# Expert matrices loaded with four neighbouring rows to a partition, and one-hot rows made a step sooner

## The chip, the cores and the metric

The kernel runs on one core of one Trainium2 chip. The time is that of the device in microseconds (us), the median of several runs; before the change it is 1736.42 us, the median of three (1735.65 to 1737.06).

## What is computed

Two blocks in a row on 256 tokens of 1024 features, in float32. The first (two layers of retention, dilated attention, gated mixing and a gated feed-forward) and most of the second (a state-space branch and a pooling branch with modulation by a condition vector) are touched by the change only through small loads. The change acts on the end of the second block, a mixture of experts:

```python
xl = post_norm(xl, mod_l[2] * out_l, ln1_g, ln1_b)          # layer_norm(alpha * x + y)
hl = modulate(xl, mod_l[3], mod_l[4])                        # x * (1 + scale) + shift
lg = hf @ w_rg + b_rg;  grp = argmax(lg)                     # one of 4 groups of 8 experts
le = (hf @ w_re[grp] + b_re[grp]);  top_v, top_i = top_k(le, 2)
w = softmax(lg)[grp] * softmax(top_v)
# each token goes to its 2 experts of 32:
def swiglu(xb, wg, wu, wd):                                  # wg, wu: 1024 x 512, wd: 512 x 1024
    return (silu(xb @ wg) * (xb @ wu)) @ wd
y = segment_sum(swiglu(...)[dest] * w, token)
xl = post_norm(xl, mod_l[5] * y, ln2_g, ln2_b)
```

## The kernel before

Everything is one program in which each of the five engines has its own function (`tensor`, `scalar`, `vector`, `gpsimd`, `sync`) with the order of its work written out by hand. Work is ordered across engines by named marks on semaphores: `then(..., key)` or `sig(...)` sets a mark when an instruction is done, `wait_ge(*at(key))` waits for it. Almost all instructions are recorded in small helpers, so a line in the profile says which kind of operation it is: L143 is a matmul, L145 a transpose on TensorE, L147 an activation, L149 tensor_tensor, L151 tensor_scalar, L153 scalar_tensor_tensor, L159 a copy, L169 a DMA issue.

**The expert stage.** The 32 experts are taken in 16 pairs. At most 64 tokens of each expert are handled in a round (`CAP`), and the tokens of the two experts of a pair stand side by side as 128 columns. For pair p:
- VectorE's `gather` makes one-hot rows `ONE` (which token stands at which place; four tensor_scalar of 128x64) and `PW`, the same with the token's weight (four more).
- TensorE's `gather` multiplies the normed tokens `X` with `ONE`: eight blocks of 128 features, in two banks (q = 0 and 1), each block as four instructions, and transposes `PW`. VectorE (q = 0, two operations) and ScalarE (q = 1, four) apply the modulation and leave the features on the partitions in `HG`.
- TensorE's `gate_up` multiplies `HG` with the gate matrices of both experts (part 0), then with the up matrices (part 1). Between the two it does `combine(p - 1)`, which adds the previous pair's result, spread over the tokens by `PWT`, and VectorE's `combined` accumulates it in `YA`.
- VectorE multiplies silu(gate) with up into `AV`; TensorE transposes `AV` in four blocks; VectorE copies them into `AT`; TensorE's `down` multiplies with the down matrices; VectorE scales the result into `OE`.

The order on TensorE is gate(p), combine(p-1), up(p), gather(p+1), transposes of the products of p, down(p). The order on VectorE is combined(p-1), `AV`, then all of `gather(p+1)` with its one-hot rows first, then the copy into `AT`, then `OE`.

**The matrices.** Each expert has three matrices of 2 MB: pair p needs loads k = 6p to 6p+5 (gate, gate, up, up, down, down). They go in turn into nine slots of 16 KB a partition (`expert_slots`). Loads 0 to 7 are issued by ScalarE during the stages before, load 8 and on by SP (`expert_loads`), each as soon as the matmuls that read the slot before are done: two loads when gate(p) is done, two when up(p) is done, two when down(p) is done. The source is read as `(k p) n -> p k n`: partition p holds rows p, 128+p, 256+p, and so on, so a gate or up matrix arrives as 1024 rows of 512 floats and a down matrix as 512 rows of 1024 floats.

**Before the experts.** `layer_norm` (VectorE: subtract and scale, times gain, plus bias on the second half of the features; GpSimd: plus bias on the first half) works in place on `X`. `routing` transposes `X` and multiplies with the router's weights `WR`, which GpSimd's `small_loads` loaded early in the first layer. The modulation vectors `modc` come from a product with `w_ada_2` and a bias that stands in `colT`.

Of the kernel before, what the change touches and what calls it, by code (L numbers as in the profile page):

```python
# [287 lines left out]
def program(nc, A, out):  # L288
    st = ExitStack()
    with st:  # L290
# [71 lines left out]
        s_col = [sem("col0_in"), sem("col1_in"), sem("col0b_in")]  # L362
# [107 lines left out]
        GSA, GSB = view(0, 8, 256), fold(ring[:, SLOT:SLOT + 2048], 8)  # L470
        dcol, ghalf, bhalf = stat[:, 128:144], stat[:, 144:160], stat[:, 240:256]
# [21 lines left out]
        PT1 = view(8192, 2, 512)  # L493
        BN = stat[:, 160:184].rearrange("p (t a b) -> p t a b", t=2, a=2)
# [63 lines left out]
        def expert_load(e, r, k):  # L558

            p, j = divmod(k, 6)  # L560
            name = ("w_expert_gate_2", "w_expert_up_2", "w_expert_down_2")[j // 2]
            src = A[name][0, 2 * p + j % 2].rearrange("(k p) n -> p k n", p=P)
            e.dma_start(fold(slot_for(r, k), 8 if j < 4 else 4), src).then_inc(*landed(s_w[r][k % len(s_w[r])], ("ew", r, k)))
# [3 lines left out]
        def tensor(t):  # L567
# [45 lines left out]
            def layer(l):  # L613
# [205 lines left out]
                def ada_sums(u):  # L819
                    bk = take(("ada", u), ("modc", u))  # L820
                    t.wait_ge(*at("am", u, "kept"))
                    if u // 2 in (2, 5):
                        t.matmul(bk, C("selbc"), AD[u % 2], True, True).then_inc(*sig(s_mm, ("ada", u)))
                        return
                    for c in range(4):
                        made = t.matmul(bk[:, 2 * c:2 * c + 2], AD[u % 2][:, tok(c)], C("selc"), True, True)
                    made.then_inc(*sig(s_mm, ("ada", u)))
# [332 lines left out]
            def routing():  # L1160
                bkl = take(("lg",), ("lg", "kept"), hold=True)
                for i in range(2):
                    for q in range(2):
                        bk = take(("hm", i, q), ("hm", i, q, "kept"))
                        for h in range(2):
                            t.wait_ge(*at("ln", 1, i, h))
                        for k in range(4):
                            made = t.transpose(bk[:, tok(k)], X[:, i, tok(4 * q + k)], ident)
                        made.then_inc(*sig(s_turn, ("hm", i, q)))
                    t.wait_ge(*at("wrg_in"))  # L1170
                    t.wait_ge(s_small[6], 64)
# [12 lines left out]
            def experts(r, s_done):  # L1184

                def gather(p):
                    i = p % 2
                    for q in range(2):
                        bk = take(("hg", r, p, q), ("hg", r, p, q, "kept"))
                        t.wait_ge(*at("one", r, p))  # L1190
                        for k in range(4):
                            c = tok(4 * q + k)
                            made = summed(bk[:, tok(k)], [(X[:, x, c], ONE[:, i, x, :]) for x in range(2)])
                        made.then_inc(*sig(s_done, ("hg", r, p, q)))
                    bk = take(("pw", r, p), ("pw", r, p, "kept"))
                    t.wait_ge(*at("pwd", r, p))
                    for x in range(2):
                        made = t.transpose(bk[:, tok(x)], PW[:, i, x, :], ident)
                    made.then_inc(*sig(s_done, ("pw", r, p)))

                def gate_up(p):
                    i = p % 2
                    for part in range(2):
# [5 lines left out]
                        t.wait_ge(*at("hg", r, p, 0, "kept"))  # L1209
                        t.wait_ge(*at("hg", r, p, 1, "kept"))  # L1210
                        for k in range(8):
                            t.matmul(bk[0:64, :], HG[:, i, k, 0:64], wa[:, k, :], k == 0, k == 7)
                            made = t.matmul(bk[64:128, :], HG[:, i, k, 64:128], wb[:, k, :], k == 0, k == 7)
# [4 lines left out]
                def down(p):  # L1218
                    i = p % 2
# [4 lines left out]
                    made.then_inc(*sig(s_done, ("av", r, p)))  # L1224
                    k0 = 6 * p + 4
# [519 lines left out]
        def vector(v):  # L1745
# [118 lines left out]
            def modulated_by(u):  # L1864
# [9 lines left out]
                then(v.tensor_tensor(o, fold(bk[:, 0:8], 4), bc(colT[:, 2, 4 * u:4 * u + 4], 2), ALU.add), *([] if plus else [("modc", u)]))  # L1874
# [451 lines left out]
            def layer_norm(name, tiles, x):  # L2326
# [7 lines left out]
                for i in tiles:  # L2334
# [3 lines left out]
                    for h in range(2):  # L2338
                        then(v.tensor_tensor(x[:, i, half(h)], x[:, i, half(h)], GB[:, 0, half(h)], ALU.mult), ("lng", name, i, h))
                    v.wait_ge(*at("ln_row", name, 1))  # L2340
                    v.wait_ge(*v.latest)
                    then(v.tensor_tensor(x[:, i, half(1)], x[:, i, half(1)], GB[:, 1, half(1)], ALU.add), ("ln", name, i, 1))
# [104 lines left out]
            def experts(r, s_done):  # L2447
# [9 lines left out]
                def gather(p):  # L2457
# [14 lines left out]
                    then(made, ("pwd", r, p))  # L2472
                    o = HG[:, i, 0:4, :]
# [7 lines left out]
                def combined(p):  # L2481
                    for x in range(2):
                        for h in range(2):
                            y, bk = YA[:, x, half(h)], B("ya", r, p, h, x)
                            v.wait_ge(*at("ya", r, p, h, x))
                            if r == 0 and p == 0:
                                then(v.stt(y, X[:, x, half(h)], ALPHA, bk, ALU.mult, ALU.add), ("ya", r, p, h, x, "kept"))
# [7 lines left out]

                gather(0)
                for p in range(16):
                    i = p % 2
                    if p:
                        combined(p - 1)  # L2500
# [4 lines left out]
                    then(v.tensor_tensor(AV, SIL, B("gu", r, p, 1), ALU.mult), ("gu", r, p, 1, "kept"), ("av_made", r, p))  # L2505
# [46 lines left out]
        def gpsimd(g):  # L2552
# [34 lines left out]
            def small_loads():  # L2587
# [7 lines left out]
                g.dma_start(WR[:, :, 0:4], A["w_router_group_2"][0].rearrange("(k p) n -> p k n", p=P)).then_inc(*landed(s_small[5], ("wrg_in",)))  # L2595
                for k in range(4):
                    g.dma_start(WR[:, :, 4 + 8 * k:12 + 8 * k], A["w_router_expert_2"][0, k].rearrange("(k p) n -> p k n", p=P)).then_inc(*landed(s_small[6]))
# [83 lines left out]
            def layer_norm(name, tiles, x):  # L2681
                i0, i1 = tiles[0], tiles[-1] + 1
                power(RV[:, i0:i1], i1 - i0, ("var", name, i0), ("rstd", name, i0))
                for i in tiles:
                    g.wait_ge(*at("ln_row", name, 1))
                    g.wait_ge(*at("lng", name, i, 0))
                    then(g.tensor_tensor(x[:, i, half(0)], x[:, i, half(0)], GB[:, 1, half(0)], ALU.add), ("ln", name, i, 0))
# [14 lines left out]
            g.dma_start(colrow[0:48, 2, :], fl(A["b_ada_2"][0])).then_inc(*landed(s_col[1]))  # L2702
            layer(0)
# [200 lines left out]
```

## Time and profile before

| | |
|---|---|
| Median of 3 runs | 1736.42 us |
| The profiled execution | 1734.91 us, span 1733.0 us |
| TensorE busy | 1623.3 us, 94% |
| VectorE, ScalarE, GpSimd busy | 45%, 34%, 27% |
| Read from HBM | 395.15 MB, 229 GB/s over the span |
| Expert stage | from about 1222 us to the end |

Times inside the profile are microseconds from the span's start. PE is TensorE's matmuls, PEld its weight loads, DVE is VectorE, ACT ScalarE, POOL GpSimd, SP the engine that issues most DMAs; SPq, ACTq are their queues. `ps<-arena` names what is written and read: `ps` is PSUM, `arena`, `ring` and `rows` are the large tensors in SBUF in which the named views lie (`ring` and parts of `arena` and `rows` hold the nine slots). A float32 matmul shows as two instructions.

### The profile page before, as it was taken

The page shows a single profiled execution, that of the slowest core. Times are in us where ns is not written, and L with a number is a line of the kernel's source. Part 1 is how long each engine was busy: PE and PEld are TensorE (multiplying, and loading weights), DVE is VectorE, ACT ScalarE, POOL GpSimd, SP SyncE. Part 2 cuts the span into 40 slices and gives each one's busy share as a digit, 9 for nine tenths or more (in the row PEclk, how much of TensorE's full clock was granted, in tenths as well). Part 3 has the DMA queues.
Part 4 walks back from the last instruction along what each step waited for, and adds up shares of the span by engine and source line. Part 5 has one row for each costly group of instructions (what it writes and reads, how often), then busy time and mean ns, then how long its engine had stood idle before and what let it go on. Part 6 is the DMA issues. An engine that isn't in the chain of part 4 may idle for free.

```text
span 1733.0 us, 23951 instructions
## 1 busy us (share of the span) xinstructions
PE 1623.3 (94%) x9717; PEld 1212.2 (70%) x9717; DVE 773.7 (45%) x1320; ACT 584.6 (34%) x1046; POOL 463.0 (27%) x291
## 2 busy tenths in 40 slices
PE   7999999989999999989999999996899999989996
PEld 5888998869889888878768888985434343343342
DVE  4644433266443332697756564466222222222323
ACT  3543444335434444555445564331100000000000
POOL 3532554433325444100245563432000000000000
PEclk9999999999999999999999999997999999999998
DMA  7644996545449874333223437569699999999992
GB/s 256 213 136 132 265 245 219 174 166 162 137 137 292 248 267 170 107 85 95 68 74 98 107 114 241 166 201 339 232 391 397 392 393 396 392 394 395 392 395 101
DMA packets 305444, 397.83 MB, mean 230 GB/s; under 512 B 6565, under 2 KB 195265, under 8 KB 304944
## 3 DMA queue, kind: packets, MB, share of 16 engines
q1 hardware_dynamic: 293424, 365.45, 63.3%
q10 hardware_dynamic: 9136, 20.85, 3.3%
q0 software_dynamic: 2768, 9.93, 1.7%
q8 instruction: 80, 1.31, 0.3%
q14 instruction: 36, 0.29, 0.1%
HBM read 395.15 MB, written 1.05 MB: 229 GB/s over the span
## 4 chain that ended last, share of the span: by engine, by line
PE 83%; DVE 10%; DMA 3%; issue 2%; ACT 1%; POOL 1%; SPq 0%; DVEq 0%; ACTq 0%; POOLq 0%
PE ps L143 81%; DVE arena L153 2%; DVE arena L149 2%; PE ps L145 2%; DVE split_r L149 2%; DMA ring<-in_w_branch_b 1%; DVE arena L159 1%; ACT split_r L147 1%; DVE arena L151 1%; DMA ring<-in_w_in 1%; DMA X<-in_x 0%; ACT arena L147 0%; DVE X L153 0%; POOL split_r L149 0%; POOL stat L149 0%
## 5 line engine op out<-in xcount | busy, mean ns | idle before, releaser
L143 PE MATMUL ps<-arena_r,split_r 128*128 128x256 f32 (+1 forms) x2984 | 462.0, 289 | 5.8 <-ACT split_r L147 3.3
L149 POOL TENSOR_TENSOR split_r<-ring,split_r 128x1024 fp32r<-128x1024 f32 (+1 forms) x142 | 334.3, 2356 | 336.9 <-ACT split_r L147 327.8
L143 PEld LDWEIGHTS ps<-arena_r,split_r 128*128 128x128 f32 x2984 | 395.5, 189 | 23.1 <-issue 14.4
L147 ACT ACTIVATE split_r<-ring 128x1024 fp32r<-128x1024 f32 (+1 forms) x293 | 296.0, 1019 | 300.5 <-PE ps L143 213.2
L143 PE MATMUL ps<-arena 128*64 128x512 f32 (+7 forms) x1472 | 359.6, 491 | 10.1 <-DVE arena L159 5.0
L149 DVE TENSOR_TENSOR split_r<-ring,split_r 128x1024 fp32r<-128x1024 f32 (+1 forms) x151 | 214.1, 1420 | 312.6 <-ACT split_r L147 304.8
L143 PE MATMUL ps<-split_r,arena_r 128*128 128x512 f32 (+1 forms) x1520 | 342.5, 378 | 2.9 <-issue 1.7
L143 PEld LDWEIGHTS ps<-split_r,arena_r 128*128 128x128 f32 x1520 | 274.7, 188 | 51.5 <-issue 8.2
L143 PEld LDWEIGHTS ps<-arena 128*64 128x64 f32 (+2 forms) x1472 | 154.5, 156 | 169.8 <-issue 147.0
L143 PE MATMUL ps<-ring,arena 128*64 128x512 f32 (+2 forms) x768 | 211.2, 576 | 12.2 <-DVE arena L159 8.6
L143 PE MATMUL ps<-hhh_r,split_r 128*128 128x256 f32 (+1 forms) x976 | 222.7, 317 | 0.0
L147 ACT ACTIVATE arena<-ps 128x256 f32<-128x256 f32 (+4 forms) x182 | 76.6, 435 | 357.2 <-PE ps L143 352.0
L149 DVE TENSOR_TENSOR arena<-arena,ps 128x512 f32<-128x512 f32 (+1 forms) x124 | 73.4, 592 | 259.4 <-PE ps L143 224.2
L143 PEld LDWEIGHTS ps<-hhh_r,split_r 128*128 128x128 f32 x976 | 162.9, 190 | 12.2 <-issue 0.6
L143 PEld LDWEIGHTS ps<-ring,arena 128*64 128x64 f32 (+1 forms) x768 | 75.2, 143 | 114.3 <-issue 92.0
L169 POOL DMA_DIRECT2D rows<-in_ln_g x2 | 1.2, 608 | 490.7 <-PE ps L143 490.7
L147 ACT ACTIVATE arena<-ps,modc 128x128 f32<-128x128 f32 x92 | 34.5, 457 | 258.2 <-PE ps L143 235.9
L143 PE MATMUL ps<-arena,X 128*128 128x128 f32 x640 | 81.2, 286 | 35.9 <-DVE arena L151 35.9
L143 PEld LDWEIGHTS ps<-arena,X 128*128 128x128 f32 x640 | 77.2, 200 | 50.8 <-DVE arena L151 39.1
L149 DVE TENSOR_TENSOR arena<-ps,rows 128x512 f32<-128x512 f32 x60 | 40.7, 690 | 132.4 <-PE ps L143 131.9
L153 DVE SCALAR_TENSOR_TENSOR arena<-ps,rows,arena 128x508 f32<-128x508 f32 (+4 forms) x104 | 69.7, 675 | 26.8 <-ACT arena L147 20.3
L149 POOL TENSOR_TENSOR arena_r<-arena,arena_r 128x256 fp32r<-128x256 f32 (+1 forms) x46 | 38.2, 832 | 159.6 <-ACT arena_r L147 151.2
(144 smaller groups left out, 1144.7 us busy)
## 6 DMA issues: line engine op xcount, KB each, us to landing
ring<-in_w_gate_up SPq DMA_DIRECT2D x88, 512.0 KB, 7.3
arena<-in_w_expert_up SPq DMA_DIRECT2D x15, 2048.0 KB, 19.2
arena<-in_w_expert_gate SPq DMA_DIRECT2D x15, 2048.0 KB, 20.1
ring<-in_w_expert_down SPq DMA_DIRECT2D x15, 2048.0 KB, 19.7
ring<-in_w_in SPq DMA_DIRECT2D x57, 512.0 KB, 5.3
ring<-in_w_expert_gate SPq DMA_DIRECT2D x13, 2048.0 KB, 16.6
arena<-in_w_ada SPq DMA_DIRECT2D x24, 1024.0 KB, 7.1
ring<-in_w_down SPq DMA_DIRECT2D x22, 1024.0 KB, 4.9
```

The source lines that it names most:

```text
L143: made = e.matmul(*a, **k)
L145: made = e.transpose(*a, **k)
L147: made = e.activation(*a, **k)
L149: made = e.tensor_tensor(*a, **k)
L151: made = e.tensor_scalar(*a, **k)
L153: made = e.scalar_tensor_tensor(**k)
L159: made = e.tensor_copy(*a, **k)
L169: made = e.dma_start(*a, **k)
```

## The change

Three things are changed. Expert matrices are read as `(q p k) n -> p q (k n)` with k = 4 (gate, up) and `(p k) n -> p (k n)` (down): four neighbouring rows to a partition, 8 KB or 16 KB in one piece. For this the features of the tokens are stored reordered: the norm before the experts writes `X` so that block k of a half holds features 4p+k, and the router's weights, the modulation bias and the product `AV` are reordered alike; the accumulation of pair 0 puts the order back. The one-hot rows of pair p+1 are made at the beginning of step p. And TensorE turns the products of p between the two halves of gather(p+1).

```diff
         def expert_load(e, r, k):
-            src = A[name][0, 2 * p + j % 2].rearrange("(k p) n -> p k n", p=P)
-            e.dma_start(fold(slot_for(r, k), 8 if j < 4 else 4), src).then_inc(...)
+            w = A[name][0, 2 * p + j % 2]
+            if j < 4:
+                o, src = fold(slot_for(r, k), 2), w.rearrange("(q p k) n -> p q (k n)", q=2, k=4)
+            else:
+                o, src = slot_for(r, k), w.rearrange("(p k) n -> p (k n)", k=4)
+            e.dma_start(o, src).then_inc(...)
...
+        in_fours = lambda x: x.rearrange("t (k p) -> t p k", k=4)
+        by_four = lambda x: x.rearrange("t (p k) -> t p k", k=4)
...
 # tensor: experts
-                gather(0)
+                for q in range(2):
+                    gather(0, q)
                 for p in range(16):
                     gate_up(p)
                     if p < 15:
-                        gather(p + 1)
+                        gather(p + 1, 0)
+                    turn_products(p)
+                    if p < 15:
+                        gather(p + 1, 1)
                     down(p)
...
 # vector: layer_norm (gain goes to LT, the add writes X reordered; gpsimd the same for half 0)
-                        then(v.tensor_tensor(x[:, i, half(h)], x[:, i, half(h)], GB[:, 0, half(h)], ALU.mult), ...)
+                        then(v.tensor_tensor(LT[i][:, half(h)], x[:, i, half(h)], GB[:, 0, half(h)], ALU.mult), ...)
-                    then(v.tensor_tensor(x[:, i, half(1)], x[:, i, half(1)], GB[:, 1, half(1)], ALU.add), ...)
+                    then(v.tensor_tensor(in_fours(x[:, i, half(1)]), by_four(LT[i][:, half(1)]), by_four(GB[:, 1, half(1)]), ALU.add), ...)
...
 # vector: experts (ones_of is the one-hot part of the former gather)
+                ones_of(0)
                 gather(0)
                 for p in range(16):
                     i = p % 2
+                    if p < 15:
+                        ones_of(p + 1)
                     if p:
                         combined(p - 1)
...
-                    then(v.tensor_tensor(AV, SIL, B("gu", r, p, 1), ALU.mult), ...)
+                    then(v.tensor_tensor(in_fours(AV), by_four(SIL), by_four(B("gu", r, p, 1)), ALU.mult), ...)
...
 # gpsimd: small_loads (five loads of the router's weights become ten)
-                g.dma_start(WR[:, :, 0:4], A["w_router_group_2"][0].rearrange("(k p) n -> p k n", p=P))...
-                for k in range(4):
-                    g.dma_start(WR[:, :, 4 + 8 * k:12 + 8 * k], A["w_router_expert_2"][0, k].rearrange("(k p) n -> p k n", p=P))...
+                for q in range(2):
+                    rows_of = lambda x: x[512 * q:512 * q + 512].rearrange("(p k) n -> p k n", k=4)
+                    g.dma_start(WR[:, 4 * q:4 * q + 4, 0:4], rows_of(A["w_router_group_2"][0]))...
+                    for k in range(4):
+                        g.dma_start(WR[:, 4 * q:4 * q + 4, 4 + 8 * k:12 + 8 * k], rows_of(A["w_router_expert_2"][0, k]))...
...
+            g.dma_start(fold(BP, 4), A["b_ada_2"][0][3 * D:5 * D].rearrange("(u p k) -> p u k", u=4, k=4))...
```

Left out above: the first accumulation reads `X` and the product with the same two reorderings; `ada_sums` and `modulated_by` take reordered weights and the bias `BP` for the eight modulation blocks that the experts use; TensorE waits for the two halves of `HG` separately.

## Rows read from the trace of the kernel before

**Rows 1.** The page: busy time by engine, and GB/s in 40 slices

```profile
PE 1623.3 (94%) x9717; PEld 1212.2 (70%) x9717; DVE 773.7 (45%) x1320; ACT 584.6 (34%) x1046; POOL 463.0 (27%) x291
...
GB/s 256 213 136 132 265 245 219 174 166 162 137 137 292 248 267 170 107 85 95 68 74 98 107 114 241 166 201 339 232 391 397 392 393 396 392 394 395 392 395 101
```

**Rows 2.** Chain that ended last, expert stage: start us, us, what

```profile
1424.19 0.69 DVE arena L149
1425.59 3.84 PE ps L143 x32
...
1430.86 24.63 PE ps L143 x104
1455.58 0.69 DVE arena L149
...
1708.90 8.16 PE ps L143 x34
```

**Rows 3.** Waits, 1230 to 1733: us in total, times, longest us

```profile
PE ps L143 <- DVE arena L151: 22.7, 15, 1.5
...
PE ps L143 <- DVE arena L159: 12.5, 16, 0.8
```

**Rows 4.** Timeline of one step: start us, us, engine, line, operation, out<-in

```profile
1424.79 1.62 DVE L151 TENSOR_SCALAR arena<-cst_sb,arena 128x64 f32<-128x64 f32 x8
...
1425.59 3.84 PE L143 MATMUL ps<-arena,X 128*128 128x128 f32 x32 [1.51 <-DVE arena L151]
1427.67 0.69 DVE L149 TENSOR_TENSOR arena<-ps,modc 128x512 f32<-128x512 f32 x1 [1.25 <-PE ps L143]
1428.40 0.69 DVE L149 TENSOR_TENSOR arena<-arena,modc 128x512 f32<-128x512 f32 x1
...
1429.26 0.82 PE L145 MATMUL ps<-cst_sb,arena 128*128 128x128 f32 x6
...
1430.12 0.69 DVE L159 COPY arena<-ps 128x512 f32<-128x512 f32 x1 [1.02 <-PE ps L145]
```

**Rows 5.** Windows of 3 us: busy by engine, PEclk, DMA share, GB/s

```profile
1418.00:1421.00 3.00, 3.00 (x18) 1.00 (x16) 0.00 (x0) 0.00 (x0) 0.00 (x0) 1.00 1.05 386
...
1466.00:1469.00 3.00, 3.00 (x16) 1.01 (x14) 0.65 (x1) 0.00 (x0) 0.00 (x0) 1.00 1.02 408
```

**Rows 6.** Timeline of SP's DMA issues in the expert stage

```profile
1228.90 0.37 SPq L169 DMA_DIRECT2D arena<-in_w_expert_up  x1
...
1298.95 13.84 SPq L169 DMA_DIRECT2D ring<-in_w_expert_gate  x2
...
1585.18 12.51 SPq L169 DMA_DIRECT2D ring<-in_w_expert_gate  x2
```

**Rows 7.** DMA packets between 1200 and 1733

```profile
DMA packets 78114, 189.19 MB, mean 355 GB/s; under 512 B 1529, under 2 KB 1529, under 8 KB 78084
```

**Rows 8.** Window of 1 us in which constants (1344 KB, 10.5 KB a partition) land

```profile
18.00:19.00 1.00, 1.00 (x5) 0.60 (x4) 0.86 (x6) 0.98 (x2) 0.00 (x0) 1.00 1.02 430
```

**Rows 9.** Timeline of VectorE before the experts: slowest 128x512, a norm's end

```profile
1165.52 2.48 DVE L149 TENSOR_TENSOR arena_r<-arena,arena_r 128x512 fp32r<-128x512 f32 x1 [0.71 <-ACT arena_r L147]
...
1196.23 2.96 DVE L149 TENSOR_TENSOR X<-X,rows 128x512 f32<-128x512 f32 x3
```

**Rows 10.** Timeline of GpSimd in the first layer

```profile
55.34 3.49 POOL L169 DMA_DIRECT2D small<-in_w_router_expert  x4
58.85 3.64 POOL L149 TENSOR_TENSOR split_r<-ring,split_r 128x768 fp32r<-128x768 f32 x2
66.53 2.59 POOL L149 TENSOR_TENSOR split_r<-ring,split_r 128x768 fp32r<-128x768 f32 x1 [4.04 <-ACT split_r L147]
```

**Rows 11.** Chain that ended last, stage before the experts

```profile
1128.13 5.49 DMA ring<-in_w_branch_b
...
1138.75 12.76 DMA ring<-in_w_branch_b
```

More of the change, by code:

```diff
@@ L1169, in routing @@
                         made.then_inc(*sig(s_turn, ("hm", i, q)))
[L1170 to L1171 removed]
+                    t.wait_ge(s_small[5], 32)
+                    t.wait_ge(s_small[6], 128)
                     for k in range(8):
@@ L1184, in experts, with gather @@
             def experts(r, s_done):
-                def gather(p):
+                def gather(p, q):
                     i = p % 2
-                    for q in range(2):
-                        bk = take(("hg", r, p, q), ("hg", r, p, q, "kept"))
-                        t.wait_ge(*at("one", r, p))
-                        for k in range(4):
-                            c = tok(4 * q + k)
-                            made = summed(bk[:, tok(k)], [(X[:, x, c], ONE[:, i, x, :]) for x in range(2)])
-                        made.then_inc(*sig(s_done, ("hg", r, p, q)))
+                    bk = take(("hg", r, p, q), ("hg", r, p, q, "kept"))
+                    t.wait_ge(*at("one", r, p))
+                    for k in range(4):
+                        c = tok(4 * q + k)
+                        made = summed(bk[:, tok(k)], [(X[:, x, c], ONE[:, i, x, :]) for x in range(2)])
+                    made.then_inc(*sig(s_done, ("hg", r, p, q)))
+                    if q == 0:
+                        return
                     bk = take(("pw", r, p), ("pw", r, p, "kept"))
@@ L1216, in gate_up, with turn_products @@
                             combine(p - 1)
-                def down(p):
-                    i = p % 2
+                def turn_products(p):
                     bk = take(("av", r, p), ("av", r, p, "kept"))
@@ L1224, in down @@
                     made.then_inc(*sig(s_done, ("av", r, p)))
+                def down(p):
                     k0 = 6 * p + 4
@@ L1873, in modulated_by @@
                 plus = u // 2 in (1, 4)
-                then(v.tensor_tensor(o, fold(bk[:, 0:8], 4), bc(colT[:, 2, 4 * u:4 * u + 4], 2), ALU.add), *([] if plus else [("modc", u)]))
+                added_to = colT[:, 2, 4 * u:4 * u + 4]
+                if u // 2 in (3, 4):
+                    v.wait_ge(*at("bp_in"))
+                    added_to = BP[:, 4 * u - 24:4 * u - 20]
+                then(v.tensor_tensor(o, fold(bk[:, 0:8], 4), bc(added_to, 2), ALU.add), *([] if plus else [("modc", u)]))
                 if plus:
@@ L2338, in layer_norm @@
                     for h in range(2):
-                        then(v.tensor_tensor(x[:, i, half(h)], x[:, i, half(h)], GB[:, 0, half(h)], ALU.mult), ("lng", name, i, h))
+                        then(v.tensor_tensor(LT[i][:, half(h)], x[:, i, half(h)], GB[:, 0, half(h)], ALU.mult), ("lng", name, i, h))
                     v.wait_ge(*at("ln_row", name, 1))
                     v.wait_ge(*v.latest)
-                    then(v.tensor_tensor(x[:, i, half(1)], x[:, i, half(1)], GB[:, 1, half(1)], ALU.add), ("ln", name, i, 1))
+                    then(v.tensor_tensor(in_fours(x[:, i, half(1)]), by_four(LT[i][:, half(1)]), by_four(GB[:, 1, half(1)]), ALU.add), ("ln", name, i, 1))
             def first_norm(i):
@@ L2455, in experts, with ones_of @@
                 v.wait_ge(*v.latest)
-                def gather(p):
+                def ones_of(p):
                     i = p % 2
@@ L2472, in gather @@
                     then(made, ("pwd", r, p))
+                def gather(p):
+                    i = p % 2
                     o = HG[:, i, 0:4, :]
@@ L2486, in combined @@
                             if r == 0 and p == 0:
-                                then(v.stt(y, X[:, x, half(h)], ALPHA, bk, ALU.mult, ALU.add), ("ya", r, p, h, x, "kept"))
+                                then(v.stt(by_four(y), in_fours(X[:, x, half(h)]), ALPHA, by_four(bk), ALU.mult, ALU.add), ("ya", r, p, h, x, "kept"))
                             else:
@@ L2686, in layer_norm @@
                     g.wait_ge(*at("lng", name, i, 0))
-                    then(g.tensor_tensor(x[:, i, half(0)], x[:, i, half(0)], GB[:, 1, half(0)], ALU.add), ("ln", name, i, 0))
+                    then(g.tensor_tensor(in_fours(x[:, i, half(0)]), by_four(LT[i][:, half(0)]), by_four(GB[:, 1, half(0)]), ALU.add), ("ln", name, i, 0))
             def norm_rows(name, a, b):
@@ L2702, in gpsimd @@
             g.dma_start(colrow[0:48, 2, :], fl(A["b_ada_2"][0])).then_inc(*landed(s_col[1]))
+            g.dma_start(fold(BP, 4), A["b_ada_2"][0][3 * D:5 * D].rearrange("(u p k) -> p u k", u=4, k=4)).then_inc(*landed(s_col[3], ("bp_in",)))
             layer(0)
```

21 lines of the change are left out of this document (12 added, 9 removed).

## The prediction

> **What bounds the kernel now.** I began with the page. TensorE is busy in 94% of the span, but over the last eleven of the 40 slices, where the experts run, the DMA engines move 391 to 398 GB/s, far above the 230 GB/s mean [rows 1]. So there are two candidates for the bound in that stage, and the stage is where the change acts. The chain of waits of the expert stage settles who sets the end: it repeats one pattern per pair of experts, from 1424.19 to 1455.58, a step of 31.39 us, and in it there is no transfer at all: 24.63 us of down, gate, combine and up matmuls, then VectorE, then the gather, then VectorE again [rows 2]. The totals of waits say the same: TensorE waits 22.7 us in 15 waits for the one-hot rows (L151) and 12.5 us in 16 waits for the copy of the turned products (L159) [rows 3]; no wait for a transfer is in that answer. A reader should see one step in the timeline [rows 4]: the eight one-hot operations start at 1424.79, behind the product of gate and up, and the gather starts at 1425.59 when the first four are done, 1.5 us after the up matmuls ended; the transposes start at 1429.26 and take 0.82, and the copy at 1430.12 holds TensorE for another 0.78.
>
> But the transfers are close behind. In stretches in which only gate and up matrices land (rows of 512 floats, 2 KB) the rate is 386 GB/s; where only down matrices land (4 KB rows) it is 408 [rows 5]. A pair is six matrices of 2.097 MB, 12.58 MB: 4 x 5.43 + 2 x 5.14 = 32.0 us, against a step of 31.39. The transfers are therefore already 2% too slow, and the kernel lives on its lead of nine slots. The issues on SP show it: the same two gate issues come at 1298.95 and, nine steps later, at 1585.18, which is 286.2 us where nine steps are 282.5; SP has slipped 3.7 us because the queue is full [rows 6]. So neither half of this change is enough alone, and this is the point of the prediction: with a shorter step on TensorE the old transfers would become the bound, and with faster transfers alone nothing would happen.
>
> **The change part by part.**
> *One-hot rows a step sooner, gather in two halves around the turning of the products.* The one-hots of the next pair now run before the combine, during the down matmuls, so the 15 waits of 1.51 go: 22.7 us. In the new order TensorE goes from up directly to half of the gather, 16 instructions, half of 3.84 = 1.92 us. The product of gate and up (0.69) ends by then, with 1.1 us to spare. Then come the four turns, the other half, and the two turns of the weights: all of it 3.84 + 0.82 = 4.66 us from the end of up. VectorE's work meanwhile: its two operations on the first gathered half start 2.08 after the gather's start (1427.67 against 1425.59) and end 1.42 later [rows 4], at 3.5, and the copy (0.69) ends at 4.2, before 4.66. So the second wait is covered too, with 0.4 us to spare: 15 x 0.78 = 11.7 us. (The 16th, in the last pair, stays: no gather is left there.) Together 34.4 us. Back-to-back groups of matmuls still have about 0.1 us between them where the wait was, 15 x 0.1 = 1.5. This leaves 32.9 us. The new step is 31.39 - 2.2 = 29.2 us.
> *The transfers.* 29.2 us for 12.58 MB asks for 431 GB/s. What do rows of 8 KB (gate, up) and 16 KB (down) give? All packets of the stage are of 2 or 4 KB [rows 7], so I draw a line through the two rates. Per engine, 2048 bytes take 16 x 2048 / 386 = 84.9 ns and 4096 take 16 x 4096 / 408 = 160.6; a fixed part of 9.2 ns and 75.7 per 2 KB. Then 8 KB take 312 ns (420 GB/s) and 16 KB take 615 (426): an estimate, 422 GB/s over a pair, 29.8 us. The nearest row to it is the microsecond in which rows of 10.5 KB (constants) land, 430 [rows 8]; the bound below is the present mix, 393 (12.58 MB in 32.0 us). With 422 the transfers are slower than TensorE by 0.6 us a step, 9 us in 15 steps, and the nine slots hold that: the first load behind the preloaded ones is issued at 1228.90 [rows 6], 87 loads or 182.5 MB are left, and the last must be there when the last down matmuls start, at 1708.90 [rows 2] less 31.9, 1677. That needs 182.5 / (1677 - 1231) = 409 GB/s. At 422 the last lands at about 1664. So at 409 or more TensorE alone sets the end.
>
> *The reordering of features.* The second half of a norm's add (VectorE), the first half (GpSimd), the product (16 times) and the first accumulation now write with 512 bytes between neighbours. No row shows such a write. Below, they cost nothing more than now; above, I take the slowest VectorE operation on 128x512 in the trace, 2.48 us, for 0.69 [rows 9]. At 2.48 the product would end 0.6 us after the half gather, 15 x 0.6 + 1.8 in the last pair = 11 us, and two norm adds in the chain would add 2 x 1.8 = 3.6. The three VectorE operations behind a norm take 2.96 together now [rows 9]. I take 0.5 us for the norm and nothing for the product, as 1.1 us of cover absorbs a 2.5-fold duration.
>
> The rule that speaks against the change is in the Trainium skill, Advanced Engine Details and Errata, section Memory Cachelines: an access that leaves its 16-byte line each time pays a penalty, with no size given. No row of this trace shows such a write. By the rule the time would be nearer to the second rival's 1718 than to 1704.5.
>
> *Small loads.* Five more issues on GpSimd: four such take 3.49 us now, two operands' low parts (3.64) stand behind them [rows 10]. The halves are smaller, so 5 x 0.5 to 5 x 0.87: 2.5 to 4.4 us of delay, once, on an engine that idles 4.04 us soon after [rows 10]; 0 to 2 us, I take 0.5. The bias load is one issue of 0.5 us, far from its use.
> *The preloaded matrices.* Eight of them share the engines with the last weights before the experts. One such load lies in the chain beside an expert's matrix: 12.76 us, where its like took 5.49 alone [rows 11]. It waits for the whole matrix already (5.4 us), so longer packets can't make it much worse: -7.3 to +2, I take 0.
>
> Sum: 34.4 - 1.5 - 0.5 - 0.5 = 31.9 us. Of the profiled execution (1734.91, span 1733.0) this leaves 1703.0, span 1701.1. The median of the runs is 1.5 above it: 1736.42 - 31.9 = 1704.5.
>
> **The rivals.**
> *Rows are cut or are no faster (12 in 100).* The descriptors stay at today's rates, the one-hots' gain is real. TensorE's 29.2 outruns 393 GB/s, the lead is used up at about the tenth pair, and then each pair waits some 2.8 us for its gate matrices. The last load lands at 1231 + 182.5 / 0.393 = 1695, and the last down starts there, 13 to 16 us before 1708.90: 1720 to 1723. For it: only two lengths were seen in this stage. Against: [rows 8].
> *Strided writes are dear (11 in 100).* As worked out, 31.9 - 14 = 18 gained: 1718.
> *Slower: long rows hurt the memory side (6 in 100).* Sixteen engines read neighbouring 8 KB pieces of one matrix at once, instead of 2 KB pieces, and meet in the same banks. Below 182.5 / (1708.90 - 1231) = 382 GB/s the time is above today's, and at 360 the last load lands at 1738, 29 us late: 1765. Against: [rows 8], and that 4 KB beat 2 KB.
> *More than forecast (6 in 100).* The preloaded matrices let the weights through sooner, up to 7 us: 1697.
>
> **How the numbers follow.** Forecast 65 in 100, 1704.5, itself 1700 to 1710. The range of 1697 to 1722 takes in the strided writes and most of the first rival and leaves out about 12 in 100. A measurement of this kernel can tell 0.2%, 3.5 us. Faster 0.92: all but the slower case and 2 in 100 for the first two rivals at once, which together take back nearly all; same 0.02, for these; slower 0.06.
>
> **What would show it.** The chain of the expert stage has steps of 29.2 us, with neither L151 nor L159 among its waits but for the first and the last pair; packets of the stage of 8 KB and over, rates of 418 to 428 GB/s; no wait of TensorE for a matrix; SP no longer held for 6.9 us by an issue (13.84 for two now, [rows 6]). A wait for an expert's matrix from the middle pairs on would say that the first rival holds; L149 before the turns, that the writes are dear.

## The result, and the profile after

The changed kernel takes 1708.16 us (median of 4 runs, 1706.24 to 1713.51), the kernel before beside it 1736.74 (4 runs, 1735.65 to 1738.08): ratio 0.984, 95% interval 0.9817 to 0.9863. Forecast were 1704.5 in a range of 1697 to 1722. The gain is 28.6 us instead of 31.9. The profiled execution took 1707.69 us, span 1705.8, against a span of 1733.0 before.

The page of the changed kernel, for [rows 1]: busy time, and GB/s in 40 slices.

```profile
PE 1627.1 (95%) x9717; PEld 1214.9 (71%) x9717; DVE 779.8 (46%) x1320; ACT 584.7 (34%) x1046; POOL 468.0 (27%) x297
...
GB/s 259 206 135 133 253 266 213 184 119 200 141 91 300 249 250 228 127 77 99 75 50 100 101 108 135 297 170 260 166 415 421 424 421 421 424 422 425 421 424 119
```

Ten slices that stood at 391 to 397 now stand at 415 to 425. In the expert stage the chain, for [rows 2], holds nothing but TensorE from the second pair to the last:

```profile
1418.60 0.44 PE ps L145 x4
1419.04 1.79 PE ps L143 x16
...
1421.04 26.51 PE ps L143 x120
1447.56 0.44 PE ps L145 x4
```

A step is 28.96 us (31.39 before). The waits of TensorE from 1230 on, for [rows 3]; the two that are left are those of the last pair:

```profile
PE ps L145 <- DVE arena L149: 1.2, 1, 1.2
PE ps L143 <- DVE arena L159: 0.8, 1, 0.8
```

The timeline of one step, for [rows 4]:

```profile
1445.51 2.05 PE L143 MATMUL ps<-arena,X 128*128 128x128 f32 x16
...
1445.69 1.05 DVE L149 TENSOR_TENSOR arena<-arena,ps 128x512 f32<-128x512 f32 x1 [6.41 <-PE ps L143]
...
1447.39 0.60 PE L145 MATMUL ps<-cst_sb,arena 128*128 128x128 f32 x4
1447.59 0.69 DVE L149 TENSOR_TENSOR arena<-ps,modc 128x512 f32<-128x512 f32 x1 [0.85 <-PE ps L143]
1447.83 1.95 PE L143 MATMUL ps<-arena,X 128*128 128x128 f32 x16
...
1448.93 0.68 DVE L159 COPY arena<-ps 128x512 f32<-128x512 f32 x1
```

The strided product takes 1.05 us where it took 0.69, and ends at 1446.74, before the transposes at 1447.39. The copy ends at 1449.61; the down matmuls that read it start at 1449.93. Both waits are covered, as forecast.

But the chain has a new piece ahead of the experts, in the norm:

```profile
1180.29 17.11 DMA rows<-in_ln_b
...
1197.42 1.04 DVE X L149
```

The timeline of VectorE says the same, for [rows 9]; the norm stands still for its gain (2.07 us) and then for its bias (4.98 us):

```profile
1191.14 1.29 DVE L149 TENSOR_TENSOR arena<-X,rows 128x512 f32<-128x512 f32 x2 [2.07 <-DMA rows<-in_ln_g]
1197.42 1.04 DVE L149 TENSOR_TENSOR X<-arena,rows 128x512 f32<-128x512 f32 x1 [4.98 <-DMA rows<-in_ln_b]
```

The span divides at two marks: the start of the last norm's first operation, and the gather of pair 0. All columns are worked out from the traces' times. The first column moves by itself: in the 14 profiles an operation of GpSimd near 500 us, with the same code ahead of it but for the small loads, starts between 498.5 and 504.8.

| kernel | start to norm | norm and routing | experts | span |
|---|---|---|---|---|
| before | 1180.96 | 33.77 | 518.27 | 1733.0 |
| after | 1182.95 | 40.64 | 482.21 | 1705.8 |
| difference | +1.99 | +6.87 | -36.06 | -27.2 |

So the experts gave 36.1 us, more than forecast, and 8.9 were lost ahead of them, where I had put 1.0. The experiments take these three columns in turn.

### The profile page after: what moved, and what is told of

Same layout as the page of the kernel before. It is cut to its first block, busy times and chain, and to the rows that moved or that the text cites. A ratio compares the mean times of both kernels' runs of the same rounds, so it can differ in the third digit from the quotient of the medians.

```text
span 1705.8 us, 23942 instructions
## 1 busy us (share of the span) xinstructions
PE 1627.1 (95%) x9717; PEld 1214.9 (71%) x9717; DVE 779.8 (46%) x1320; ACT 584.7 (34%) x1046; POOL 468.0 (27%) x297
## 3 DMA queue, kind: packets, MB, share of 16 engines
HBM read 395.16 MB, written 1.05 MB: 232 GB/s over the span
## 4 chain that ended last, share of the span: by engine, by line
PE 86%; DVE 7%; issue 3%; DMA 2%; POOL 2%; ACT 1%; ACTq 0%; DVEq 0%; POOLq 0%
PE ps L143 84%; DVE arena L153 2%; PE ps L145 2%; DVE arena L149 1%; DVE split_r L149 1%; DMA rows<-in_ln_b 1%; POOL split_r L149 1%; POOL small L169 1%; DMA ring<-in_w_in 1%; DMA X<-in_x 0%; ACT split_r L147 0%; ACT arena L147 0%; DVE X L153 0%; DVE arena L159 0%; POOL arena_r L149 0%
## 5 line engine op out<-in xcount | busy, mean ns | idle before, releaser
L143 PE MATMUL ps<-ring,arena 128*64 128x512 f32 (+2 forms) x768 | 214.7, 584 | 4.4 <-DVE arena L149 2.4
L149 DVE TENSOR_TENSOR arena<-arena,ps 128x512 f32<-128x512 f32 (+1 forms) x124 | 79.4, 640 | 235.3 <-PE ps L143 200.4
L143 PEld LDWEIGHTS ps<-arena,X 128*128 128x128 f32 x640 | 77.3, 198 | 27.3 <-issue 23.8
```

The source lines that it names most:

```text
L143: made = e.matmul(*a, **k)
L149: made = e.tensor_tensor(*a, **k)
```

## The experiments

Theory: TensorE's two waits are gone because of the order, long rows are what lets the transfers keep up, and the loss ahead of the experts has two causes of its own. In the table, each kernel's median against the kernel before in the same study, and the stretches of its profiled execution.

| kernel | median us | ratio, 95% interval | norm | experts |
|---|---|---|---|---|
| order_only | 1728.9 | 0.9955 (0.9942 to 0.9969) | 33.71 | 510.51 |
| old_order | 1751.1 | 1.008 (1.0056 to 1.0104) | 40.78 | 520.90 |
| late_ones | 1737.4 | 1.001 (0.9996 to 1.0025) | 40.69 | 510.05 |
| whole_gather | 1723.4 | 0.9912 (0.9884 to 0.994) | 40.78 | 494.50 |
| short_all | 1734.2 | 0.9991 (0.9977 to 1.0004) | 37.82 | 510.79 |
| rows_late | 1737.4 | 1.0007 (0.9995 to 1.0019) | 40.78 | 509.90 |
| rows_4_4 | 1723.4 | 0.9935 (0.9918 to 0.9952) | 39.77 | 492.53 |
| rows_4_16 | 1715.4 | 0.9891 (0.9873 to 0.9908) | 40.38 | 487.30 |
| rows_first8 | 1706.1 | 0.982 (0.9796 to 0.9844) | 34.35 | 482.47 |
| early_rows | 1704.0 | 0.9811 (0.9788 to 0.9833) | 34.35 | 482.54 |
| ada_copy | 1705.0 | 0.982 (0.9793 to 0.9847) | 40.07 | 482.08 |
| best | 1699.3 | 0.9783 (0.9757 to 0.9808) | 34.35 | 481.75 |

### The two halves of the change, each alone

**Order alone.** The kernel before with only its order changed (`ones_of(p + 1)` ahead of `combined(p - 1)`, `turn_products(p)` between the two halves of the gather), rows of 2 and 4 KB and features in the old order.

> The kernel before with the change of order alone: one-hot rows a step sooner, the products turned between the two halves of the gather; matrices still in rows of 2 and 4 KB, features not reordered. Theory (both halves are needed): TensorE's step could be 28.96 us, but the transfers give 393 GB/s, so after some ten pairs TensorE waits for gate matrices, 2 to 3 us a pair; gain 13 to 17 us, about 1721. Rival (the transfers had room, the long rows bring nothing): the whole gain of the expert stage, 36 us, about 1701.

Measured 1728.86 (1726.28 to 1730.47), a gain of 7. Its chain, where it goes over from TensorE to the transfers:

```profile
1411.71 12.36 PE ps L143 x57
1424.07 26.02 DMA ring<-in_w_expert_gate
```

The waits of TensorE in its expert stage:

```profile
PE ps L143 <- DMA ring<-in_w_expert_gate: 9.9, 5, 2.6
PE ps L143 <- DMA arena<-in_w_expert_gate: 8.9, 3, 3.7
```

Steps are 28.96 us until 1411, the seventh pair; then come waits for gate matrices, as the prediction's first rival describes, but three pairs sooner than it puts them. The mechanism is right; the gain is only half of what I expected (below).

**Long rows alone.** The changed kernel in the old order, on both engines:

```diff
                     if p < 15:
                         gather(p + 1, 0)
+                        gather(p + 1, 1)
                     turn_products(p)
-                    if p < 15:
-                        gather(p + 1, 1)
```

and `ones_of(p + 1)` back behind the product.

> The changed kernel with the old order: one-hot rows behind the product, both halves of the gather before the products are turned; long rows and reordered features stay. Theory (TensorE sets the step, transfers alone bring nothing): steps of 31.4 us and the losses before the experts stay, so 1708.2 + 36.4 = about 1744, slower than the kernel before. Rival (the transfers held the old kernel): little lost against the changed kernel, 1708 to 1715.

Measured 1751.07 (1748.78 to 1752.91): 15 us slower than before the change. Its chain around the product:

```profile
1439.44 1.03 DVE arena L149
1440.47 0.58 DVE arena L151 x4
...
1446.37 24.63 PE ps L143 x104
...
1471.09 1.03 DVE arena L149
```

The step is 31.65 where the old one was 31.39: the strided product takes 0.35 more, which nothing covers in this order, and the four one-hot operations in the chain 0.09 less (0.58 for 0.67). The experts lose 2.6 us by this against the kernel before. The rest of the loss stands ahead of them: 7.0 us in the norm, 3.9 in the modulation (both below), and some 4.5 us that this profile lost elsewhere ahead of the norm. Expected were 1744; the kernel is 7 us above that, 2.3 of them in the experts. So neither half is worth much alone (-7 and +15 us), and together they bring 28.6.

### Which of the two waits brings how much

**One-hot rows late, gather halved**: only `ones_of(p + 1)` moved back behind the product.

> The changed kernel (long rows, gather in two halves around the turns) with the one-hot rows of the next pair made behind the product of gate and up again, where they were before the change. This prices the first wait alone. Theory: TensorE waits for the first one-hots in each of 15 steps, 1.51 us as before the change and 0.35 more because the product in front of them writes strided and takes 1.04 instead of 0.69: 15 x 1.86 = 27.9, 1736 us and steps of 30.8; the second wait stays covered (the copy is ready 0.4 us before the second half of the gather ends). Rival: the two waits are one, what is not waited for at the first is waited for at the second, and taking the one-hots early alone brings less than 1.51 a step: 1725 or below.

Measured 1737.37 (1735.66 to 1741.19). The chain:

```profile
1402.70 0.58 DVE arena L151 x4
...
1403.32 2.05 PE ps L143 x16
...
1434.11 2.05 PE ps L143 x16
```

Steps of 30.79, 1.83 more than in the changed kernel, which is 27.5 us in 15 steps; the stage is 27.84 us longer, against 27.9 worked out.

**One-hot rows early, gather whole**: only `gather(p + 1, 1)` moved ahead of `turn_products(p)`.

> The changed kernel (long rows, one-hot rows early) with the whole gather in front of the turns of the products again. This prices the second wait alone. Theory: TensorE waits for the copy of the turned products in each step, 0.78 us, nothing else changes since the strided product has 3.8 us of cover: 15 x 0.78 = 11.7, 1720 us and steps of 29.75. Rival: the two halves bring no more than they cost (an extra switch between gather and turns, 0.1 us twice a step): 1708 to 1711.

Measured 1723.36 (1719.4 to 1726.58). The chain:

```profile
1403.48 0.67 PE ps L145 x6
...
1404.18 0.70 DVE arena L159
...
1404.92 28.37 PE ps L143 x136
1433.29 0.67 PE ps L145 x6
```

Steps of 29.81, 0.85 more, which is 12.8 us in 15 steps; the stage is 12.3 us longer, against 11.7. The two waits are separate and their prices add up: 1.83 + 0.85 = 2.68 a step, and old_order, which has both waits, is 2.69 a step above the changed kernel.

### The transfers

**Short rows again, as four transfers for each matrix.** The changed kernel with every matrix in four `dma_start` of one row to a partition and block.

> The changed kernel, but every matrix is loaded in four transfers that take one row of each partition, so the packets are 2 and 4 KB again while features and order stay as changed. Theory: the expert stage is bound by 393 GB/s or a little less, 20 us longer than in the changed kernel; the waits for the norm's rows before the experts (2.1 and 5.0 us) go, since nothing long stands in their way; about 1722 to 1727. Rival (packet length has no part): 1708 or, if the norm's rows come sooner, 1701.

Measured 1734.22 (1729.18 to 1740.54), more than expected. The edit has a side effect that I had missed: the two last matrices loaded beforehand are now eight issues on ScalarE, in front of the activations that the routing waits for. From its timeline:

```profile
1195.61 11.71 ACTq L169 DMA_DIRECT2D ring<-in_w_expert_gate  x8
1207.36 2.90 ACT L147 ACTIVATE arena<-ps,modc 128x128 f32<-128x128 f32 x8 [21.93 <-issue]
```

So the run can't price the rows alone, and three others replace it, with one transfer for each matrix, whose source is read in shorter rows (`(q p k) n -> p q (k n)` with k = 1 or 2). Their matrices don't stand in the order of the features, so their results aren't those of the computation; bytes, matmuls and order of work are the same.

**Rows of 2 and 4 KB from k = 8 on.**

```diff
+            if k >= 8:
+                if j < 4:
+                    o, src = fold(slot_for(r, k), 8), w.rearrange("(q p k) n -> p q (k n)", q=8, k=1)
+                else:
+                    o, src = fold(slot_for(r, k), 4), w.rearrange("(q p) n -> p q n", p=P)
```

> The changed kernel, but all loads from k = 8 on are read in rows of 2 and 4 KB as before the change (so wrong features, same work). It is the run with four times as many transfers without their side effect on ScalarE. Theory: transfers bind at 393 GB/s; 182.5 MB take 464 us where the stage leaves 444 between the first of these issues and the last down matmuls: 20 us late, and some 7 more as in the kernel with the new order alone: 1728 to 1735. Rival: the long rows are not what lets the stage run at 28.96 a step, the landing time of a single transfer or the lead does: 1708 to 1715.

Measured 1737.43 (1736.81 to 1739.4), 2.4 us above the range that the theory gave. The stage takes 509.90, nearly that of order_only (510.51).

**Rows of 4 KB for gate and up, 16 KB for down.**

> The changed kernel, but gate and up matrices from k = 8 on are read in rows of 4 KB (wrong features, same work), down matrices in 16 KB as now. Theory, from the line through the rates of packets (408 GB/s at 4 KB, 426 at 16 KB): 4 x 5.14 + 2 x 4.92 = 30.4 us a pair, 414 GB/s, and 182.5 MB take 441 us of the 444 there are: no loss, 1708 to 1710. Rival: the slots are too few for transfers that are 1.4 us a pair slower than TensorE, and waits come up from the middle pairs on: 1715 to 1722.

Measured 1715.39 (1713.73 to 1718.16), the rival's number but not its waits from the middle pairs on. The timeline of TensorE has one wait for a gate and one for an up matrix, both in the last pair:

```profile
1663.70 10.72 PE L143 MATMUL ps<-arena 128*64 128x512 f32 x40 [1.69 <-DMA arena<-in_w_expert_gate]
1676.48 8.79 PE L143 MATMUL ps<-arena 128*64 128x512 f32 x32 [2.07 <-DMA arena<-in_w_expert_up]
```

**Rows of 4 KB for all.**

> The changed kernel, but all matrices from k = 8 on are read in rows of 4 KB (gate and up with wrong features, same work). Theory: 408 GB/s, 182.5 MB take 447 us of the 444 there are: 3 us late and a little of the landing time, 1711 to 1716, so that two neighbouring rows to a partition would have been nearly enough. Rival: as soon as TensorE waits for transfers it loses more than the deficit, since the time in which a full ring stands still is not made up: 1718 or more.

Measured 1723.38 (1719.18 to 1725.15), again the rival's number. The rates of the four kernels, from the counts of packets between 1245 and 1640, in the order rows_late, rows_4_4, rows_4_16, after, a fence each:

```profile
DMA packets 63912, 155.67 MB, mean 394 GB/s; under 512 B 1188, under 2 KB 1188, under 8 KB 63894
```

```profile
DMA packets 40634, 161.57 MB, mean 409 GB/s; under 512 B 1238, under 2 KB 1238, under 8 KB 40615
```

```profile
DMA packets 31196, 163.95 MB, mean 415 GB/s; under 512 B 1255, under 2 KB 1255, under 8 KB 27832
```

```profile
DMA packets 18139, 167.02 MB, mean 423 GB/s; under 512 B 1271, under 2 KB 1271, under 8 KB 1271
```

The line through two rates gave 408, 414 and 422 for the last three. The rates are right within 1 GB/s; what was wrong is the rate that is needed. The stage takes 509.9, 492.5, 487.3 and 482.2 us; 182.5 MB at the first three rates are 463.2, 446.2 and 439.8 us, and what remains is 46.7, 46.3 and 47.5, nearly a constant: the stage lasts as long as the transfers and 47 us. TensorE's own 482.2 then ask for 182.5 / 435 = 419 GB/s, not 409. Changed kernel 423: 1% to spare.

### The loss ahead of the experts

**Gain and bias rows issued earlier.** GpSimd's waits and `norm_rows(1, ...)` moved ahead, in front of two of its tensor operations and of the operand splits behind them. The issue of the gain stands at 1109.79 where it was at 1179.67, 70 us sooner.

> The changed kernel with the two transfers of the first norm's gain and bias issued some 60 us sooner, in the gap after the branch_a weights, so that they don't share the engines with experts' matrices. Theory (the bias row's transfer, 10.0 us before and 17.1 after, was held up by the long packets of the preloaded matrices, and this cost 6.9 us): the waits of 2.1 and 5.0 us go, 1701 to 1702. Rival (the norm is slower because it writes with strides and its two halves collide): no gain, 1708.

Measured 1703.97 (1702.71 to 1704.52), 4.2 us less than the changed kernel where 6 to 7 were expected. The norm stretch is 34.35 us, 6.3 less, without a wait for a transfer.

**The matrices loaded beforehand in short rows.** The diff of rows_late with `k < 8` in place of `k >= 8`. It asks why the rows land late.

> The changed kernel, but the eight matrices loaded beforehand (k < 8) are read in rows of 2 and 4 KB as before the change, in one transfer each as before (their features then stand in the wrong order, so the first expert pairs compute with other weights; the work is the same). This asks whether it is their packets that hold up the norm's rows. Theory: the transfer of the bias rows (4 KB packets on GpSimd's queue) takes turns with them packet by packet, so it lands in 10.0 us again instead of 17.1, the norm takes 6.9 us less, and the branch weights in front take some 2.8 us more, as before the change: 1708.2 - 6.9 + 2.8 = 1704.1 us. Rival: the norm is longer for another reason (its strided adds, the detour over LT) and the landing stays at 17: 1708 to 1711.

Measured 1706.06 (1699.81 to 1709.26), against 1704.1 by the theory; the median can't tell this from 1708, the trace can. The issue table between 1165 and 1215, in KB and us to landing, of the changed kernel and then of this one:

```profile
ring<-in_w_expert_down ACTq DMA_DIRECT2D x2, 2048.0 KB, 15.1
...
rows<-in_ln_b POOLq DMA_DIRECT2D x1, 512.0 KB, 17.1
```

And with short rows:

```profile
ring<-in_w_expert_down ACTq DMA_DIRECT2D x2, 2048.0 KB, 16.3
...
rows<-in_ln_b POOLq DMA_DIRECT2D x1, 512.0 KB, 9.8
```

The bias rows are the same 128 packets of 4 KB in both. Beside matrices in 2 and 4 KB packets they land after 9.8 us, beside 8 and 16 KB packets after 17.1, while the matrices land a little sooner (15.1 for 16.3). The norm stretch is 34.35 again. That is what turns by packets look like: whoever has the short packets gets the smaller share. The Trainium skill, DMA: Bandwidth & Descriptors, section Queues, rings and completion order, says that an engine goes round its queues at the granularity of packets. By that rule, the traces agree; its packet is a group of descriptors, and no run here shows whether that is what the profile counts as one.

**Contiguous weights in the modulation.** The changed kernel reads reordered sums as TensorE's weights; here VectorE reorders when it copies them.

```diff
-                then(v.copy(AD[u % 2], B("am", u)), ("am", u, "kept"))
+                if u // 2 in (3, 4):
+                    then(v.copy(in_fours(AD[u % 2]), by_four(B("am", u))), ("am", u, "kept"))
```

with `AD[u % 2][:, tok(c)]` as the operand on TensorE.

> The changed kernel with one edit: the modulation sums of the eight blocks that the experts use are reordered when VectorE copies them out of PSUM, so that TensorE reads contiguous weights again in the four stages of the modulation where it now reads them with 16 bytes between neighbours (eight weight loads of 1.94 us together where they took 0.98). Theory: these strided weight loads cost 4 x 0.96 = 3.9 us, all of it on TensorE's path; expected 1704.3 us against 1708.2, the group of eight loads back at 0.98, and VectorE's copies 0.35 us longer beside TensorE's work. Rival: the weight loads lie beside matmuls or a transfer ends these stages anyway, and the shift of the two traces there is only noise: 1708. Second rival: the strided copy stands in the path instead and costs 4 x 0.35 = 1.4: 1705.7.

Measured 1704.96 (1703.97 to 1708.39), 3.2 less. The group of eight weight loads in the changed kernel, and then here:

```profile
553.46 1.94 PEld L143 LDWEIGHTS ps<-cst_sb,arena 128*128 128x128 f32 x8
```

```profile
553.33 0.98 PEld L143 LDWEIGHTS ps<-cst_sb,arena 128*128 128x128 f32 x8
```

Such a group stands four times in the trace. Between the same two operations of GpSimd on either side of them (at 500.24 and 707.24 in the changed kernel), before takes 203.15 us, the changed kernel 207.00, ada_copy 203.14: 3.86 for 4 x 0.96, all of it on the path. The other profiles say the same: 207.00 or 207.01 in the nine more with the strided read, 203.15 in the two without.

**Both repairs.**

> The changed kernel with both repairs: gain and bias rows of the norm before the experts issued some 60 us earlier (alone: 1703.97, 4.2 us less) and contiguous weights in the modulation. Theory: the two are in different stages and add up: 1708.2 - 4.2 - 3.9 = 1700.1 us. Rival: a transfer behind both (the branch weights, or the expert matrices loaded beforehand) takes one of the two back: 1704.

Measured 1699.28 (1696.78 to 1700.12), 37 us below the kernel before. Its interval lies below that of the changed kernel. What the second repair brings beside early_rows is 4.7 us, 3.2 in ada_copy alone; neither difference is resolved by its own interval, and 3.86 from the traces lies between.

## Why the prediction was right, and where it was not

**Right: the bound, and that the halves need each other.** TensorE set the end through two waits, with the transfers 2% behind it. Order alone: 7 us gained; long rows alone: 15 lost; both: 28.6. (The prediction reads eleven slices at 391 to 398 GB/s in [rows 1]; they are ten at 391 to 397, which changes nothing.) That 28.6 came so near to 31.9 is in part luck: 3.2 us more than forecast in the experts, and 3.6 us that I can't assign (below), stand against 10.2 us ahead of the experts that the prediction put at nothing.

**Waits removed, 34.4 less 1.5 forecast, 36.1 measured.** The step that failed is the 0.1 us between groups, 15 times. By the chains, of the old step of 31.39, matmuls and transposes are 24.63 + 3.84 + 0.67 = 29.14 and 2.25 is VectorE and the hand-overs. The new step is 28.96, less than 29.14: where a group no longer starts from rest, 0.18 goes too. 2.25 + 0.18 = 2.43 a step, 36.5 in 15; the longer product in the last pair takes 0.35 back. Where the prediction has 0.1 us between groups, the chains have none. late_ones and whole_gather measured the two waits at 27.84 (0.35 a step of it the strided product) and 12.3.

That the whole stage, too, gave 36.1 is a coincidence. From the first gate matmuls to the last down matmuls it is 487.12 us before and 450.93 after, 36.2 less. Ahead of that, 1.7 us went too, since TensorE waits for the two halves of `HG` separately; the prediction put no price on this. Before, the first gate matmuls stood still for the second half:

```profile
1221.78 13.95 PE L143 MATMUL ps<-arena 128*64 128x512 f32 x64 [1.47 <-ACT arena L147]
```

In the changed kernel they follow the transposes without a wait, at 1228.93. And behind the last down matmuls' start 1.8 us came back, 1.7 of them in these matmuls. Before, and then in the changed kernel:

```profile
1708.90 7.09 PE L143 MATMUL ps<-ring,arena 128*64 128x512 f32 x32 [0.79 <-DVE arena L159]
```

```profile
1679.86 8.78 PE L143 MATMUL ps<-ring,arena 128*64 128x512 f32 x32 [0.79 <-DVE arena L159]
```

The granted clock is 0.54 between 1682 and 1684, the lower of the two levels for most of it, and 1.00 throughout the same group before. TensorE had waited twice shortly ahead of the group, 1.20 and 0.79 us. The same two waits stand in ada_copy and best, which have the same code there and take 7.09, and in early_rows, which takes 8.78, so I count this as chance and no effect of the change.

**Rates of long rows.** 422 GB/s as an estimate, 423 measured.

**Rate needed.** 409 was too low; the runs say 419. By the same sum with the changed kernel's own times (first issue 1236.06 and 2.1 us more, as the sum has it, last down matmuls 1679.86) it is 182.5 / 441.7 = 413: the stage got 4 us shorter than forecast. Then there are 1.05 MB of gain and bias rows of the last norm, which make it 183.5 / 441.7 = 415. And not only the last down matrices have a due time: the gate matrices of the last pair do too (83 loads, 174.1 MB, by 1659.54), and there TensorE waited in rows_4_16, at 415 GB/s. The remaining 4 GB/s I can't assign. The outcome of the change didn't hang on it, since 423 is above both; order_only's, rows_late's and the two 4 KB runs' expectations did, and missed their ranges by 2 to 7 us. The first rival's 1720 to 1723 is low for the same reason: rows_late, that case in the flesh, took 1737, though its experts also start 10.8 us later than those of the kernel before.

**Strided writes.** 0.69 became 1.04 to 1.05 us for the product, hidden by the first half gather; a norm add went from 1.65 to 1.92 and 2.00. The 0.5 for the norm was 0.58 (34.35 against 33.77). My upper end of 2.48 was far off. The Trainium skill, Advanced Engine Details and Errata, section Memory Cachelines, names a penalty when each access goes to another line, and gives no size. By that rule, the trace agrees: there is a penalty, here +50% on a write in VectorE and +98% on TensorE's weight loads. What the second rival's 1718 needed, a product over 1.8 us, isn't there.

**Small loads: 0.5 forecast, 0.6 measured.** Ten loads instead of five put the operation behind them at 61.20 instead of 58.85, and TensorE waits for it:

```profile
63.17 2.33 PE L143 MATMUL ps<-split_r,arena_r 128*128 128x384 f32 x12 [0.44 <-POOL split_r L149]
```

Between the same two groups of TensorE on either side (from 42.05 to 66.28; from 42.76 to 66.36 before) it is 24.23 us instead of 23.60. The wait, 0.41 to 0.49 us, stands in all twelve profiles with ten loads, and not in order_only and before, which have five.

**Matrices loaded beforehand: 0 forecast, bounds -7.3 to +2; the norm lost 6.3.** This is the largest of the steps that failed. I asked who waits for these transfers, the branch weights in the chain, and not who else is in flight with them. The gain and bias rows are issued in the same microseconds, in shorter packets (4 KB), and had no room: before the change the bias landed at 1188.3 and the add that reads it began at 1188.58. early_rows and rows_first8 each give the 6.3 back. The branch weights themselves may have gained: the last of them is waited for 5.5 to 6.4 us in the ten profiles with long rows, 7.1, 6.6 and 6.5 in three with short ones, but 4.4 in order_only, also short. This stays open.

**Modulation: not in the prediction.** The diff reads reordered weights at one place, I named it in a half sentence and priced nothing: 3.86 us. I had looked for strided writes only; a strided read by TensorE cost more than all the strided writes together.

**The rest of the first column.** +3.9 for the modulation and +0.6 for the small loads are effects of the change. +1.7 is a stretch at 370 us in which 16 matmuls took 7.12 us instead of 5.43: the granted clock between 369 and 376 is 0.76 of full speed and 0.50, the lower level, between 370 and 372, where it is 1.00 in best; TensorE had waited 2.3 us ahead of them in both. The same group is at 5.43 in early_rows and at 7.12 in order_only, and the code there is the same in all of them, so this is chance. Up to 42 us the changed kernel's profile is 0.7 us ahead, which is chance too, since order_only, early_rows, ada_copy and best stand later there than before. What is left, -3.6, lies between the operation at 707.24 and the norm. That stretch is 475.7 to 478.1 us in the ten profiles with long rows ahead, and 479.3, 479.1, 478.3 and 474.7 in the four with short ones: not told apart, and open.

The account of the span: -36.1 experts, +6.9 norm (6.3 waits for the gain and bias rows, 0.6 writes), +3.9 modulation, +0.6 small loads, +1.7 and -0.7 chance, -3.6 open: -27.2 or -27.3 with the rounding.

## What to carry to other kernels

Where two resources are within a few per cent of each other, change both at once and price each alone; a repair of one can look worthless, or harmful, by itself. When a transfer is made more efficient with longer packets, list everything that is in flight beside it, on all queues, with its slack: the small load with short packets pays. When a layout is permuted, price every reader and writer of it, TensorE's weight reads first, and let a copy that is there anyway do the reordering.

## What the hardware showed that was not expected

- Fixed and proportional part of a packet: the rates at 2 and 4 KB (386, 408) gave those of 4 KB throughout (409), 4 and 16 KB (415), and 8 and 16 KB (423) within 1 GB/s.
- Share by packets: the same 512 KB in 4 KB packets land after 9.8 us beside a queue with 2 and 4 KB packets and after 17.1 beside one with 8 and 16 KB.
- Weights read with 16 bytes between neighbours: 0.24 us for a load of 128x128 (1.94 for eight), 0.12 (0.98) when contiguous.
- A float32 write of 128x512 on VectorE with 512 bytes between neighbours: 1.04 us for 0.69.
- Issues can hold their engine: eight on ScalarE in short_all took 11.71 us, where four of the same size took 2.39 at 1148.65, and the activations behind them came late. That a full queue holds them is my reading; no row shows the queue. In the changed kernel too, SP still spends 11.44 us on two gate issues, so the forecast that SP would be held no longer was wrong, at no cost:

```profile
1561.82 11.44 SPq L169 DMA_DIRECT2D ring<-in_w_expert_gate  x2
```
